# Two stages with fewer products on TensorE: a convolution mixer by one level of Strassen's scheme, and attention heads that scale probabilities on VectorE and fetch the rotated halves by DMA

## The chip, the cores and the metric

The kernel runs on one core of a Trainium2 chip. The time is device microseconds for one execution of the whole program; lower is better. Everything is computed in float32.

## The reference, cut to what matters

The program is a block of three mixers (window attention, a gated linear recurrence, a delta-rule recurrence) followed by two further layers on 1040 tokens (16 learned ones and the 1024 of the input), each a mixer and a mixture of 64 experts. The change touches the mixers of those two layers:

```python
def short_conv_mixer(hn, w_in, conv_w, w_out):      # hn: 1040 x 1024, w_in: 1024 x 3072
    bcu = hn @ w_in
    b, c, u = jnp.split(bcu, 3, axis=-1)
    z = c * u
    z = lax.conv_general_dilated(z, conv_w, ..., padding=((2, 0),), feature_group_count=z.shape[-1])  # 3 taps
    return (b * z) @ w_out

def apply_rope(x, cos, sin):
    x1, x2 = x[..., :half], x[..., half:]
    return jnp.concatenate([x1 * cos - x2 * sin, x1 * sin + x2 * cos], axis=-1)

# attention of layer 2: 8 heads, queries and keys of 128 plain + 64 rotated columns, values of 128
q = (cq @ w_uq).reshape(bsz, t, 8, 128 + 64)
q_rope = apply_rope(q[..., 128:], cos, sin)
s = (q_nope @ k_nope.T + q_rope @ k_rope.T) * scale, causal
o = softmax(s, axis=-1) @ v
```

## The kernel before

The program is a chain of phases. A phase holds its tiles and semaphores, runs one program on each engine, and ends in a barrier of all engines. Within a phase each engine works through its own list in order and waits on semaphores. The order of the work is written by hand. SyncE (SP) issues the loads; at the end of a phase's list it issues the first loads of the next one (`next_loads`). Activations lie transposed in one big tile `all__arena` (feature on the partitions, token along the row).

**`conv_mixer` (phase cm, tiles `cm__...`).** The features of the output come in 8 tiles `j` of 128, each with three sets `s` (b, c, u). The tokens are cut in three (`CUTS`: 352, 352 and 336 columns). For each `j` and cut, TensorE makes 3 products (b, c, u), each a sum over 8 tiles `k` of the input feature: 8 x 3 x 3 x 8 = 576 matmuls (line 1514). In the trace a float32 matmul of 128 rows shows as two MATMUL records and two LDWEIGHTS records. ScalarE copies b and c out of PSUM (lines 1529, 1530), VectorE multiplies c by u (L1542), and when a whole `j` is there it applies the three taps (L1545 and twice L1547) and the gate b (L1550). Two PSUM groups of three banks alternate. The weights of tile `j` (1.5 MB) are loaded two tiles ahead into one of two buffers; those of tile 0 are loaded by the phase before, `first_out`, in the list of SyncE between the store of row tile 2 and the load of row tile 4.

**`heads` (phase hd, tiles `hd__...`).** The eight heads are done in four pairs `j`. For a pair, TensorE first runs 14 jobs (`job`, L1674): four for the plain queries (`qn`), four for the rotated ones (two halves of the tokens, each once with the weights as they are, `qa`, and once with weights whose halves are exchanged, `qb`), each 3 matmuls of 512 columns, and six for the keys (`kn`), each 2 matmuls of 352 or 336 columns. VectorE takes each result out of its PSUM bank (`job_out`): for `qa` it multiplies by the cosines (L1837), for `qb` by the sines and adds (L1839, L1840). There are four banks, so job n waits until job n-4 was taken out. The values follow (L1684, 256 columns). Then come 8 units `n`, one for each block of 128 queries, the longest first (i = 7 down to 0, with 16 + 128(i+1) keys). TensorE's list for them is `score(n+1)`, then for both heads `turn(n, h)` (transposes of the probabilities, L1727) and for both heads `mix(n, h)` (probabilities times values, L1737). `mix` ends with one more matmul, of `ones` by a diagonal matrix `dg` that holds the reciprocals of the row sums (L1739), which spreads them over all partitions. `score(n+1)` waits until both exponentials of unit n are done, since it writes the banks that these read.

ScalarE's list is `evacuate(n-1, 0)` (copies of the turned probabilities, L1798, L1802), `exponentials(n, 0)` (L1785), `evacuate(n-1, 1)`, `exponentials(n, 1)`. VectorE's list is `biggest(n)` (mask L1858, maximum L1864, L1867), `output(n-1)` (copy of the spread reciprocals L1885, product with the mixed values L1886), `diagonals(n)` (reciprocal L1878, diagonal L1879). Before the last `turn` and `mix` of a pair, TensorE already does the first two jobs of the next pair (`EARLY`).

## Time and profile before

| | |
|---|---|
| time, median of 3 runs | 3213.69 us (3211.97 to 3217.08) |
| the profiled execution, its own time | 3214.27 us |
| its span, first to last instruction | 3212.5 us |
| mean granted TensorE clock | 0.931 of 2.4 GHz |
| busy in the span | TensorE 88%, VectorE 31%, ScalarE 18%, GpSimd 6% |
| phase cm, first to last matmul | 849.5 to 1187.6 us |
| phase hd, first matmul to last output | 2026.0 to 2471.0 us |

Times are microseconds from the start of the span unless marked ns. PE is TensorE's matmuls, PEld its weight loads (they run beside the matmuls), DVE VectorE, ACT ScalarE, POOL GpSimd, SPq the DMA queue of SyncE. The start-to-start distance of matmul records, not the duration of one, tells how fast TensorE goes, since they overlap. PEclk is the granted clock as a share of 2.4 GHz: 0.50 is the level of 1.2 GHz.

### The profile page before, as it was taken

How to read it: one execution, taken by the hardware profiler on the slowest of the kernel's cores; microseconds unless marked ns; L12 is line 12 of the kernel's file. 1: busy time of each engine (PE TensorE's matmuls, PEld its weight loads, DVE VectorE, ACT ScalarE, POOL GpSimd, SP SyncE). 2: the span in 40 equal slices, each digit the busy share in tenths (PEclk: the TensorE clock that was granted, in tenths of full speed). 3: DMA queues.
4: the chain of work that ended last, by engine and by line, in shares of the span. 5: the costliest groups of instructions: out<-in, count | busy, mean ns of one | idle time of the engine just before them, and what ended most of it. 6: DMA issues, size and time to landing. Idle time of an engine off the chain costs nothing. (4 is left out here: it accounts for less than half of the span.)

```text
span 3212.5 us, 31853 instructions
## 1 busy us (share of the span) xinstructions
PE 2825.0 (88%) x12118; PEld 1575.5 (49%) x12118; DVE 990.6 (31%) x2388; ACT 586.7 (18%) x1370; POOL 205.1 (6%) x331
## 2 busy tenths in 40 slices
PE   9999988989899989988887859899999979787882
PEld 3445588874466655533333326566656543333330
DVE  2423845544311113421110124344343442011114
ACT  0211544331000001111110113123112111111111
POOL 1000011110000000011111100000000001111110
PEclk9999988889899999988998979999999979899896
DMA  2111010002111204479999973002000549999995
GB/s 101 40 33 40 1 40 0 0 27 100 52 40 40 114 1 169 186 313 420 420 420 419 418 293 145 17 1 93 1 1 1 203 185 391 420 420 419 418 412 213
DMA packets 104902, 563.98 MB, mean 176 GB/s; under 512 B 20897, under 2 KB 21057, under 8 KB 52401
## 3 DMA queue, kind: packets, MB, share of 16 engines
q1 hardware_dynamic: 78432, 500.83, 38.9%
q0 software_dynamic: 21440, 43.51, 3.6%
...
## 5 line engine op out<-in xcount | busy, mean ns | idle before, releaser
L2005 PE MATMUL ex__h_ps<-all__arena,ex__xT 128*64 128x512 f32 x1696 | 526.8, 676 | 169.2 <-DMA all__arena<-in_w_up 113.9
L2005 PEld LDWEIGHTS ex__h_ps<-all__arena,ex__xT 128*64 128x64 f32 x1696 | 171.3, 155 | 471.4 <-issue 467.1
L1514 PE MATMUL cm__acc<-all__arena,cw__w 128*128 128x352 f32 (+1 forms) x1152 | 338.5, 457 | 2.3 <-PEq L81 2.3
L295 PE MATMUL fr__acc<-X__xT,fr__w 128*128 128x512 f32 x640 | 280.0, 598 | 7.8 <-DMA X__xT<-in_xT 7.8
L1514 PEld LDWEIGHTS cm__acc<-all__arena,cw__w 128*128 128x128 f32 x1152 | 220.2, 191 | 120.4 <-issue 4.6
L1302 PE MATMUL pb__acc<-b__w,all__arena 128*128 128x512 f32 x544 | 246.1, 607 | 12.5 <-POOL pb__eps L1256 12.5
L2033 DVE TENSOR_TENSOR ex__hs<-ex__sg,ex__h_ps 128x256 f32<-128x256 f32 x64 | 27.0, 421 | 680.6 <-ACT ex__sg L2030 680.3
L295 PEld LDWEIGHTS fr__acc<-X__xT,fr__w 128*128 128x128 f32 x640 | 121.8, 191 | 163.7 <-issue 155.4
L2005 PE MATMUL ex__h_ps<-mo__wx,ex__xT 128*64 128x512 f32 x352 | 177.0, 661 | 0.0
L1302 PEld LDWEIGHTS pb__acc<-b__w,all__arena 128*128 128x128 f32 x544 | 103.2, 194 | 132.9 <-issue 119.3
L2019 PE MATMUL ex__y_ps<-b__w,ex__hT 128*64 128x512 f32 x672 | 153.5, 598 | 1.1 <-ACT ex__hT L2036 1.1
L2030 ACT ACTIVATE ex__sg<-ex__h_ps 128x256 f32<-128x256 f32 x64 | 24.6, 384 | 656.4 <-PE ex__h_ps L2005 656.4
L1737 PE MATMUL hd__o<-all__arena 128*128 128x128 f32 (+1 forms) x704 | 102.6, 285 | 4.0 <-ACT all__arena L1802 4.0
L1542 DVE TENSOR_TENSOR cm__z<-cm__cT,cm__acc 128x352 f32<-128x352 f32 (+1 forms) x24 | 12.4, 516 | 293.2 <-ACT cm__cT L1530 293.2
L2042 DVE COPY ex__ysb<-ex__y_ps 128x512 f32<-128x512 f32 x64 | 44.3, 692 | 189.1 <-PE ex__y_ps L2019 189.1
L2154 POOL DMA_INDIRECT b__rows<-s_hn,mo__queue x60 | 60.6, 1009 | 614.9 <-PE ex__x_ps L1998 614.9
L1998 PEld LDWEIGHTS ex__x_ps<-mo__ident,b__rows 128*128 128x128 f32 x512 | 63.2, 195 | 66.2 <-issue 66.2
L1737 PEld LDWEIGHTS hd__o<-all__arena 128*128 128x128 f32 (+1 forms) x704 | 88.1, 190 | 15.5 <-ACT all__arena L1802 7.5
L1069 PE MATMUL fo__acc<-all__arena 128*128 128x512 f32 x192 | 88.2, 610 | 2.4 <-PEq L81 2.4
L1998 PE MATMUL ex__x_ps<-mo__ident,b__rows 128*128 128x128 f32 x512 | 75.7, 292 | 15.6 <-PEq L81 15.6
L1674 PE MATMUL hd__s<-lt__cq,lt__wq 128*128 128x512 f32 x192 | 85.1, 601 | 2.8 <-POOL hd__ones L1648 2.8
L2159 POOL DMA_INDIRECT s_ys<-ex__ysb,mo__queue x64 | 65.2, 1019 | 289.6 <-DVE ex__ysb L2042 285.9
...
## 6 DMA issues: line engine op xcount, KB each, us to landing
...
b__w<-in_w_down SPq DMA_DIRECT2D x84, 1024.0 KB, 20.5
...
```

The lines of the kernel that those rows point to most:

```text
L295: last = mm(acc[:, b, c], wbuf[:, b, k], xT[:, k, 512 * c:512 * c + 512], start=(k == 0), stop=(k == KT - 1))
L1069: last = nc.tensor.matmul(acc[:, t % 2, c], proj[:, G_T + k, P * t:P * t + P], wo[k][:, 512 * c:512 * c + 512], start=(k == 0), stop=(k == ...
L1302: last = mm(acc[:, t % 2, c], src[:, k, P * t:P * t + P], w[:, k, 512 * c:512 * c + 512], start=(k == 0), stop=(k == KT - 1))
L1514: last = nc.tensor.matmul(acc[:, u % 2, s, 0:cols], w[:, j % 2, s, k], hnT[:, k, at:at + cols], start=(k == 0), stop=(k == KT - 1))
L1674: last = mm(job_bank(n)[:, 0:cols], w[:, j % 2, k, which], src[:, k, at:at + cols], start=(k == 0), stop=(k == kt - 1))
L1737: mm(o_ps[:, h, 0:P], vv[0:r, s, h], pT[0:r, h, s], start=(a == 0), stop=(a == len(tiles) - 1))
L1998: last = nc.tensor.transpose(x_ps[:, k // 4, P * (k % 4):P * (k % 4) + P], xe[:, b, k::KT], ident[:])
L2005: last = nc.tensor.matmul(h_ps[half, b].rearrange("p (a b) -> p a b", a=2), xT[:, b, k, half], slots[n][:, :, k], start=(k == 0), stop=(k ...
L2019: last = nc.tensor.matmul(y_ps[half, c], hT[:, b, k, half], slots[n][:, k, 512 * c:512 * c + 512], start=(k == 0), stop=(k == 1))
L2042: return nc.vector.tensor_copy(ysb[:, b, 512:], y_ps[:, 1])
L2154: g.indirect_dma_start(xe[:, p % 2], None, hn_dram[:, :], bass.IndirectOffsetOnAxis(ap=queue[:, 0, p:p + 1], axis=0), bounds_check=T - 1, ...
L2159: g.indirect_dma_start(y_rows[:, :], bass.IndirectOffsetOnAxis(ap=queue[:, 1, p:p + 1], axis=0), ysb[:, p % 2], None, bounds_check=2 * T - ...
```

## The change

**`conv_mixer`.** The output is made in units (`CONV_UNITS`), each for two neighbouring output tiles and one set s: 4 x 3 = 12 units, in the order c, u, b. A unit is a product of a 2 x 2 block matrix of weights (two output tiles by two halves of the input features) and a 2 x 2 block matrix of activations (two halves of the input features by two halves of the tokens, 520 each). It is computed in the form of Strassen's scheme that has seven products and needs sums of blocks ahead of them and behind them. The halves of the tokens are cut in two again, so that a step `u` (24 of them) has seven products of 4 matmuls with 260 columns: 24 x 7 x 4 = 672 matmuls. VectorE makes four sums of weights for a unit (`weight_sums`, 128 x 512 each), four sums of activations for each half (`row_sums`, 4 x 260 columns each, once), and seven sums of 260 columns for a step, each with one operand in PSUM (`first_sums`, `last_sums`). ScalarE copies the first product of each step. The seven products of a step go through the eight PSUM banks in turn, so a product waits for the sum that reads the product eight before it. The gate and the taps work on two output tiles at once or are spread between the sums. The weights have three buffers of 1 MB, and `first_out` now loads the first three units (6 DMAs, 3 MB) where it loaded tile 0 (3 DMAs, 1.5 MB).

**`heads`.** The two `qb` jobs of a pair are gone, and the rotated queries come first. Their result is copied to `raw`; four DMAs of SyncE (32 partitions, 128 KB each) write it to `rot` with the halves exchanged (`exchange`), and VectorE forms raw x cos + rot x sin over 1024 columns in three steps behind jobs 3, 4 and 5 (`rotate`). The matmul of `ones` and `dg` is gone. VectorE instead multiplies the probabilities of a unit by the reciprocals of their row sums, in place, before they are turned (`norms`, 128 x number of keys), `turn` waits for that, and the output is a copy. `norms(n)` stands ahead of `output(n-1)` in VectorE's list. In SyncE's list `exchange(1)` and `exchange(2)` stand behind the weight loads of pairs 2 and 3, and `exchange(3)` ahead of `next_loads`. The reordered columns of the query weights are left out, so that a pair's weights are 3 instead of 4 tiles for each k.

```diff
+CONV_SETS = (1, 2, 0)
+CONV_UNITS = [(i, s) for i in range(KT // 2) for s in CONV_SETS]
+TH = T // 2
+TC = TH // 2
+HK = KT // 2
+def conv_weight(sp, D, w, loaded, n):
+    i, s = CONV_UNITS[n]
+    for m in range(2):
+        sp.dma_start(w[:, n % 3, m], D["conv_w_in_t"][2 * i + m, :, s]).then_inc(loaded[n % 3], 16)
...
+        sums = ph.sb("sums", [P, 2, 3, HK, P])
+        t4 = ph.sb("t4", [P, HK, TH])
+        z = ph.sb("z", [P, 2, 2, T + 2])
+        ub = ph.sb("ub", [P, 2, T])
+        acc = ph.ps("acc", [P, 8, 512])
...
+        M1, M5, M6, M7, M2, M4, M3 = range(7)
+        U2, W, C22, V5, C11, C21, C12 = range(1, 8)
+        bank = lambda u, x: acc[:, (7 * u + x) % 8, 0:TC]
...
+                for n in range(3, NU):
+                    sp.wait_ge(product, 14 * (n - 2))
+                    conv_weight(sp, D, w, w_loaded, n)
...
+                def mul(u, x, weight, moving, c):
+                    for k in range(HK):
+                        last = nc.tensor.matmul(bank(u, x), weight(k), moving(k, c), start=(k == 0), stop=(k == HK - 1))
+                    last.then_inc(product, 1)
...
+                for n in range(NU):
+                    r, q = n % 3, n % 2
+                    pe.wait_ge(w_loaded[r], 32 * (n // 3 + 1))
+                    a11, a12, s3, a22 = (lambda k, m=m, h=h: w[:, r, m, HK * h + k] for m, h in ((0, 0), (0, 1), (1, 0), (1, 1)))
+                    s1, s2, s4 = (lambda k, x=x: sums[:, q, x, k] for x in range(3))
...
+                        u = 2 * n + c
                         if u >= 2:
-                            pe.wait_ge(z_made, u - 1)
-                            pe.wait_ge(copied, u - 1)
-                        for s in range(3):
-                            if u == 0:
-                                pe.wait_ge(part_loaded[s], 16)
-                            for k in range(KT):
-                                last = nc.tensor.matmul(acc[:, u % 2, s, 0:cols], w[:, j % 2, s, k],
-                                                        hnT[:, k, at:at + cols], start=(k == 0), stop=(k == KT - 1))
-                        last.then_inc(done, 1)
+                            pe.wait_ge(summed, 7 * (u - 2) + C12)
+                        mul(u, M1, a11, b11, c)
+                        pe.wait_ge(s_made, 4 * n + 1)
+                        pe.wait_ge(t_made, 4 * c + 1)
+                        if u:
+                            pe.wait_ge(e1_out, u)
+                        mul(u, M5, s1, t1, c)
+                        pe.wait_ge(s_made, 4 * n + 2)
+                        pe.wait_ge(t_made, 4 * c + 2)
+                        if u:
+                            pe.wait_ge(summed, 7 * (u - 1) + V5)
+                        mul(u, M6, s2, t2, c)
+                        pe.wait_ge(s_made, 4 * n + 3)
+                        pe.wait_ge(t_made, 4 * c + 3)
+                        mul(u, M7, s3, t3, c)
+                        mul(u, M2, a12, b21, c)
+                        if u:
+                            pe.wait_ge(summed, 7 * (u - 1) + C11)
+                        pe.wait_ge(t_made, 4 * c + 4)
+                        mul(u, M4, a22, t4n, c)
+                        if u:
+                            pe.wait_ge(summed, 7 * (u - 1) + C21)
+                        pe.wait_ge(s_made, 4 * n + 4)
+                        mul(u, M3, s4, b22, c)
...
+                for u in range(2 * NU):
+                    act.wait_ge(product, 7 * u + M1 + 1)
+                    if u >= 2:
+                        act.wait_ge(summed, 7 * (u - 2) + C11)
+                    nc.scalar.copy(e1[:, u % 2], bank(u, M1)).then_inc(e1_out, 1)
...
+                def weight_sums(n, *which):
+                    r, q = n % 3, n % 2
+                    a11, a12, a21, a22 = (w[:, r, m, HK * h:HK * h + HK] for m, h in ((0, 0), (0, 1), (1, 0), (1, 1)))
+                    if 1 in which:
+                        dve.wait_ge(w_loaded[r], 32 * (n // 3 + 1))
+                        v(V.tensor_tensor(sums[:, q, 0], a21, a22, ALU.add))
+                        dve.sem_inc(s_made, 1)
...
+                def row_sums(c, *which):
+                    lo, hi = low(c), high(c)
+                    if 1 in which:
+                        v(V.tensor_tensor(t12[:, 0, :, lo], B12[:, :, hi], B11[:, :, lo], ALU.subtract))
+                        dve.sem_inc(t_made, 1)
...
+                def add(u, result, out, a, b, op=ALU.add):
+                    V.tensor_tensor(out, a, b, op).then_inc(summed, 1)
+                    dve.wait_ge(summed, 7 * u + result)
...
+                    dve.wait_ge(e1_out, u + 1)
+                    dve.wait_ge(product, 7 * u + M6 + 1)
+                    add(u, U2, u2, e1[:, u % 2], bank(u, M6))
+                    dve.wait_ge(product, 7 * u + M7 + 1)
+                    add(u, W, c21, u2, bank(u, M7))
+                    add(u, C22, c22, c21, bank(u, M5))
+                    add(u, V5, c12, u2, bank(u, M5))
...
+                    dve.wait_ge(product, 7 * u + M2 + 1)
+                    add(u, C11, c11, e1[:, u % 2], bank(u, M2))
+                    dve.wait_ge(product, 7 * u + M4 + 1)
+                    add(u, C21, c21, c21, bank(u, M4))
+                    dve.wait_ge(product, 7 * u + M3 + 1)
+                    add(u, C12, c12, c12, bank(u, M3))
...
+                def gated(n, i):
+                    v(V.tensor_tensor(z[:, i % 2, :, 2:2 + T], z[:, i % 2, :, 2:2 + T], ub[:], ALU.mult))
...
+                weight_sums(0, 1)
+                row_sums(0, 1)
+                weight_sums(0, 2)
+                row_sums(0, 2)
+                weight_sums(0, 3)
+                row_sums(0, 3, 4)
+                weight_sums(0, 4)
+                for i in range(KT // 2):
+                    nc_, nu, nb = 3 * i, 3 * i + 1, 3 * i + 2
+                    end = i == KT // 2 - 1
+                    first_sums(nc_, i, 1, 0)
+                    if i == 0:
+                        row_sums(1, 1, 2, 3, 4)
+                    last_sums(nc_, i, 1, 0)
+                    weight_sums(nu, 1, 2, 3, 4)
+                    first_sums(nc_, i, 1, 1)
+                    last_sums(nc_, i, 1, 1)
+                    first_sums(nu, i, 2, 0)
+                    last_sums(nu, i, 2, 0)
+                    weight_sums(nb, 1, 2, 3, 4)
+                    first_sums(nu, i, 2, 1)
+                    last_sums(nu, i, 2, 1)
+                    gated(nu, i)
+                    if i == 0:
+                        dve.wait_ge(taps_loaded, 16)
+                    tap(i, 0, 0)
...
+                    first_sums(nb, i, 0, 0)
+                    tap(i, 0, 1)
+                    tap(i, 0, 2)
+                    last_sums(nb, i, 0, 0)
+                    if end:
+                        tap(i, 1, 0)
+                        tap(i, 1, 1)
+                    else:
+                        weight_sums(nb + 1, 1, 2, 3, 4)
+                    first_sums(nb, i, 0, 1)
+                    if end:
+                        tap(i, 1, 2)
+                    else:
+                        tap(i, 1, 0)
+                        tap(i, 1, 1)
+                    last_sums(nb, i, 0, 1)
+                    if not end:
+                        tap(i, 1, 2)
+                    v(V.tensor_tensor(zT[:, 2 * i:2 * i + 2, 0:T], zT[:, 2 * i:2 * i + 2, 0:T], ub[:], ALU.mult))
...
-        rot = carve(512)
+        raw = ph.sb("raw", [P, SEQ])
+        rot = ph.sb("rot", [P, SEQ])
...
-        jobs = ([("qn", h, c) for h in range(2) for c in range(2)] + [(kind, 0, c) for c in range(2) for kind in ("qa", "qb")]
+        jobs = ([("qr", 0, c) for c in range(2)] + [("qn", h, c) for h in range(2) for c in range(2)]
...
+                def exchange(j):
+                    sp.wait_ge(raw_out, 2 * (j + 1))
+                    for at in range(0, P, ROPE):
+                        for a, b in ((at, at + ROPE // 2), (at + ROPE // 2, at)):
+                            sp.dma_start(rot[a:a + ROPE // 2], raw[b:b + ROPE // 2]).then_inc(exchanged, 16)
+                exchange(0)
                 for j in range(2, NPAIR):
                     sp.wait_ge(pdone, NJ * (j - 1))
                     sp.wait_ge(v_done, NV * (j - 1))
                     pre.pair(sp, j)
+                    exchange(j - 1)
+                exchange(NPAIR - 1)
...
-                    pe.wait_ge(exped, 2 * u + h + 1)
+                    pe.wait_ge(normed, 2 * u + h + 1)
...
-                        mm(o_ps[:, h, 0:P], vv[0:r, s, h], pT[0:r, h, s], start=(a == 0), stop=(a == len(tiles) - 1))
-                    pe.wait_ge(diag_done, 2 * u + h + 1)
-                    mm(o_ps[:, h, P:2 * P], ones[:], dg[:, h, u % 2], start=True, stop=True).then_inc(mixed, 1)
+                        last = mm(o_ps[:, h, 0:P], vv[0:r, s, h], pT[0:r, h, s], start=(a == 0), stop=(a == len(tiles) - 1))
+                    last.then_inc(mixed, 1)
...
-                        act.wait_ge(diag_done, 2 * (u - 2) + h + 1)
...
-                        elif kind == "qa":
-                            if j == 0:
-                                dve.wait_ge(tab_loaded, 32)
-                            v.hold(tt(qr[:, cols], job_bank(n), cosT[:, cols], ALU.mult))
                         else:
-                            v(tt(rot[:], job_bank(n), sinT[:, cols], ALU.mult))
-                            v.hold(tt(qr[:, cols], qr[:, cols], rot[:], ALU.add))
+                            v(V.tensor_copy(raw[:, cols], job_bank(n)))
+                            dve.sem_inc(raw_out, 1)
...
+                def rotate(j, step):
+                    if step == 0:
+                        if j == 0:
+                            dve.wait_ge(tab_loaded, 32)
+                        v.hold(tt(qr[:], raw[:], cosT[:], ALU.mult))
+                    elif step == 1:
+                        dve.wait_ge(exchanged, 64 * (j + 1))
+                        v.hold(tt(rot[:], rot[:], sinT[:], ALU.mult))
+                    else:
+                        v(tt(qr[:], qr[:], rot[:], ALU.add))
...
-                def diagonals(j, n):
+                def norms(j, n):
                     i, u = units[n], NB * j + n
                     p = u % 2
                     for h in range(2):
                         dve.wait_ge(exped, 2 * u + h + 1)
                         if i == NB - 1:
                             v(tt(ls[:, h, p, 0:1], ls[:, h, p, 0:1], ls[:, h, p, 1:2], ALU.add))
-                        if u >= 2:
-                            dve.wait_ge(mixed, 2 * (u - 2) + h + 1)
                         v(V.reciprocal(rl[:, h, p:p + 1], ls[:, h, p, 0:1]))
-                        V.tensor_scalar(dg[:, h, p], ident[:], rl[:, h, p:p + 1], None, ALU.mult).then_inc(diag_done, 1)
+                        keys = keys_of(i)
+                        V.tensor_scalar(pr[:, h, p, 0:keys], pr[:, h, p, 0:keys], rl[:, h, p:p + 1], None,
+                                        ALU.mult).then_inc(normed, 1)
                 def output(j, n):
                     i, u = units[n], NB * j + n
                     for h in range(2):
                         dve.wait_ge(mixed, 2 * u + h + 1)
-                        v(V.tensor_copy(ob[:, h], o_ps[:, h, P:2 * P]))
-                        tt(oT[:, 2 * j + h, P * i:P * i + P], o_ps[:, h, 0:P], ob[:, h], ALU.mult).then_inc(oout, 1)
+                        V.tensor_copy(oT[:, 2 * j + h, P * i:P * i + P], o_ps[:, h, 0:P]).then_inc(oout, 1)
...
+                        if 3 <= n <= 5:
+                            rotate(j, n - 3)
                     values_out(j, 0)
                     biggest(j, 0)
                     for g in range(1, NV):
                         values_out(j, g)
-                    diagonals(j, 0)
+                    norms(j, 0)
                     for n in range(1, NB):
                         biggest(j, n)
+                        norms(j, n)
                         output(j, n - 1)
-                        diagonals(j, n)
```

## Rows read from the trace of the kernel before

**Rows 1.** The page, its head: the span.

```profile
span 3212.5 us, 31853 instructions
```

**Rows 2.** Windows: us, busy time (count) of PE, PEld, DVE, ACT, POOL, granted clock, DMA.

```profile
850.00:854.00 4.00, 4.00 (x8) 2.25 (x8) 0.57 (x2) 0.00 (x0) 0.00 (x0) 0.50 0.80 271
...
849.50:1187.60 338.10, 338.07 (x1152) 220.18 (x1152) 44.94 (x53) 18.36 (x46) 0.00 (x0) 0.99 0.14 51
...
330.00:410.00 80.00, 76.39 (x531) 43.00 (x529) 64.25 (x156) 51.17 (x160) 2.23 (x7) 1.00 0.00 1
...
2026.00:2471.00 445.00, 423.37 (x2064) 274.46 (x2064) 190.62 (x556) 99.97 (x305) 0.39 (x2) 1.00 0.05 20
```

**Rows 3.** Groups by shape, 845 to 1195 us: count, busy, mean ns, idle before.

```profile
L1514 PE MATMUL cm__acc<-all__arena,cw__w 128*128 128x352 f32 x768 | 231.1, 463 | 2.3 <-PEq L81 2.3
L1514 PEld LDWEIGHTS cm__acc<-all__arena,cw__w 128*128 128x128 f32 x1152 | 220.2, 191 | 120.4 <-issue 4.6
...
L1547 DVE SCALAR_TENSOR_TENSOR all__arena<-cm__z,cm__taps,all__arena 128x1040 f32<-128x1040 f32 x16 | 20.8, 1301 | 0.6
L1550 DVE TENSOR_TENSOR all__arena<-all__arena,cm__bT 128x1040 f32<-128x1040 f32 x8 | 9.9, 1241 | 0.3
...
L1545 DVE TENSOR_SCALAR all__arena<-cm__z,cm__taps 128x1040 f32<-128x1040 f32 x8 | 6.1, 761 | 0.3
```

**Rows 4.** Timeline, first and last of phase cm: start, us, engine, line.

```profile
849.53 16.71 PE L1514 MATMUL cm__acc<-all__arena,cw__w 128*128 128x352 f32 x47 [2.26 <-PEq L81]
...
850.50 0.06 DVE L1536 MEMSET cm__z<- 128x4 f32 x1
...
1188.05 0.44 ACT L1529 COPY cm__bT<-cm__acc 128x336 f32<-128x336 f32 x1 [12.75 <-PE cm__acc L1514]
...
1192.88 1.24 DVE L1550 TENSOR_TENSOR all__arena<-all__arena,cm__bT 128x1040 f32<-128x1040 f32 x1
```

**Rows 5.** Timeline, VectorE elsewhere: two-source operations of other widths.

```profile
702.89 0.42 DVE L764 TENSOR_TENSOR rwc__gr<-rwc__y,V__dg 128x256 f32<-128x256 f32 x1 [0.71 <-PE rwc__y L890]
...
2043.91 0.69 DVE L1840 TENSOR_TENSOR all__arena<-all__arena 128x512 f32<-128x512 f32 x1
...
278.06 2.29 DVE L472 TENSOR_TENSOR all__arena<-all__arena,fr__cum 128x2048 f32<-128x2048 f32 x1
```

**Rows 6.** Timeline, PE in phase hd: runs of matmuls of one width.

```profile
2048.13 7.16 PE L1674 MATMUL hd__s<-lt__ckv,lt__wkv 128*128 128x352 f32 x24
...
2165.71 1.89 PE L1684 MATMUL hd__t<-lt__wkv,lt__ckv 128*128 128x256 f32 x8
...
2174.17 3.72 PE L1684 MATMUL hd__t<-lt__wkv,lt__ckv 128*128 128x256 f32 x16
...
2245.65 5.32 PE L1674 MATMUL hd__s<-lt__cq,lt__wq 128*128 128x512 f32 x12
```

**Rows 7.** Timeline, PE and ACT around the seventh unit of a pair (i = 1).

```profile
2238.87 0.18 ACT L1785 ACTIVATION_READ_ACCUMULATOR all__arena<-hd__s,hd__nm 128x1 f32 x1
...
2239.25 1.25 PE L1737 MATMUL hd__o<-all__arena 128*128 128x128 f32 x8
...
2240.43 0.49 PE L1739 MATMUL hd__o<-hd__dg,hd__ones 128*128 128x128 f32 x2
...
2240.75 0.66 PE L1708 MATMUL hd__s<-all__arena 128*128 128x144 f32 x4
...
2241.78 0.87 PE L1727 MATMUL hd__t<-hd__ident,all__arena 128*128 128x128 f32 x6
```

**Rows 8.** Timeline, PE, a mix of 18 records and what follows it.

```profile
2190.38 2.42 PE L1737 MATMUL hd__o<-all__arena 128*128 128x128 f32 x18
2192.73 0.49 PE L1739 MATMUL hd__o<-hd__dg,hd__ones 128*128 128x128 f32 x2
```

**Rows 9.** Groups by line, 2024 to 2475 us.

```profile
L1879 DVE TENSOR_SCALAR hd__dg<-hd__ident,hd__rl 128x128 f32<-128x128 f32 x64 | 18.4, 287 | 2.3
```

**Rows 10.** DMA issues: destination and source, queue, count, size, us to landing.

```profile
all__arena<-all__arena SPq DMA_DIRECT2D x2, 256.0 KB, 6.2
```

127 lines of the change are left out of this document (66 added, 61 removed).

## The prediction

> **What bounds the kernel now.** I read the page first for the span [rows 1], then windows over the two phases that change [rows 2], then the groups by shape and the timeline inside them. In the convolution phase TensorE is busy 338.07 of 338.10 us, in the heads phase 423.37 of 445.00, both near the full clock; VectorE works 44.9 and 190.6 us there, the DMA engines 14% and 5% of the time [rows 2]. Both phases are streams of matmuls, and what they lose or gain moves all that follows, since each ends in a barrier; the weights of the experts, which fill the DMA engines later, are asked for only behind those barriers. So a matmul taken out of these two phases is worth its full distance to the next, unless its replacement makes TensorE wait.
>
> **What a column costs.** 24 records of 352 columns take 7.16 us. A record's own duration is 0.463 us [rows 3], which is its columns and 0.17, so the distance is (7.16 - 0.46) / 23 = 0.291 us. For 12 records of 512 columns it is (5.32 - 0.59) / 11 = 0.430 [rows 6]. Both are 0.83 ns per column and record, which is two passes at 2.4 GHz. The narrowest run of similar width has 256 columns: 8 records, (1.89 - 0.39) / 7 = 0.214, again 0.83 ns per column; in a run of 16 records over more groups, (3.72 - 0.39) / 15 = 0.222 [rows 6]. A weight load of 0.191 us [rows 3] thus stays hidden behind 256 columns; at 128 it no longer does: 18 and 8 records take 2.35 and 1.18 us, 0.117 apart where the columns need 0.107 [rows 7, 8].
>
> **Convolution, TensorE.** Before: 1152 records of 346.7 columns on average, 332.8 us at 0.833 ns; measured 338.1, the 5.3 us more mostly the start at the lower level of the clock, 0.50 until about 854 [rows 2, 4]. After: 672 matmuls, 1344 records of 260 columns, 291.2 us. That is -41.6 us. The bounds of the seam between products: nothing, as in the 256-column run of 8, or 0.222 - 0.214 = 0.008 us a record, +10.8 us. The 352-column run crosses six groups with their semaphores at 0.291, so I take the near end, +1.5.
>
> **Convolution, VectorE.** It must not hold TensorE. An operation of two sources costs 0.42 us at 256 columns, 0.69 at 512, 1.24 at 1040, 2.29 at 2048; the one-source tap 0.76, the other two taps 1.30 [rows 3, 5]; behind each I add 0.04 for the wait on itself. Sums behind products: 24 x 7 x 0.46 = 77 us. Sums of weights: 12 x 4 x 0.73 = 35. Sums of activations: 8 x 1.28 = 10. Gates: 8 operations of 2080 columns at 2.35 = 19. Taps: 8 x (0.80 + 2 x 1.34) = 28. Together 169 us of 291, so what counts is the order. A step on TensorE lasts 7 x 1.73 = 12.1 us. Its products end at 1.7, 3.5, 5.2, 6.9, 8.7, 10.4 and 12.1; VectorE's first four sums run from 5.2 to 8.3, its last three end at 9.1, 10.9 and 12.6. The sum on which the next step depends first (V5) is there at 8.3 and wanted at 12.1 + 3.5 = 15.6. The heaviest stretch lies behind every sixth step: a tap and the gate, 1.34 + 2.35, from 12.6 to 16.3, where the next sums may start at 17.3. Four weight sums (2.9 us) fit at the other places, and they are wanted one step later. ScalarE has one copy a step. So no wait in steady state: 0.
>
> The start is tight. Matmuls begin at 849.5, VectorE is free at 850.6 behind its memsets [rows 4]. It makes the sums in pairs of 0.73 + 1.28 = 2.0 us: ready at 852.6, 854.6, 856.6. The first product runs at half the clock, 8 x 0.433 = 3.5 us, so the second wants its pair at 853.0, the third at about 855.4, the fourth at 857.2. Each is ready 0.4 to 0.8 us ahead; if the operations on three-dimensional views are slower, the loss is one or two us, and a clock that rises sooner costs as much. I take +0.3.
>
> **Convolution, the end.** From the last copy's start (1188.05) to the end of VectorE (1192.88 + 1.24 = 1194.12) it now takes 6.1 us [rows 4]: two copies, a product, three taps and the gate. After, the taps are done, and one sum and the gate remain: 0.46 + 2.35 = 2.8. That is -3.3. Convolution: -41.6 + 1.5 + 0.3 - 3.3 = -43.1 us.
>
> **Loads.** The first three units are 3 MB in place of 1.5 ahead of the load of row tile 4 in `first_out`. Three more DMAs of 512 KB delay that load by the time of 1.5 MB; the rows give 4.00 us at 271 GB/s for 1.1 MB [rows 2], so some 5.5 us. A row tile on TensorE there is 32 records of 512 columns, 13.7 us, and tile 4 is two tiles off: hidden. Later units are asked for two units ahead, 48 us. Without that cover: +5.5, once.
>
> **Heads, the jobs.** Two jobs of 3 matmuls fewer in each of 4 pairs: 4 x 12 records x 0.430 = -20.6 us. VectorE's share is 0.69 + 1.28 behind jobs 3 to 5, under the 2.58 us of a job, so no bank is late. The exchange: four DMAs of 128 KB; the nearest row is a pair of 256 KB with 6.2 us to landing [rows 10]. At the first pair `raw` is ready after two jobs and its copy, and VectorE asks for the result behind job 4, 2.5 jobs or 7 us later; there TensorE can go on for four jobs before a bank is missing, 2.6 + 3 x 1.2 = 6 us more. So 13 us of cover at the first pair, 15 at the others, where the two early jobs come ahead of the last turn. Behind the waiting VectorE stand the outputs of later jobs, nothing else. Bounds: 0, or at a landing of 20 us 4 x 6 = +24 us. I take 0. On SyncE `exchange(3)` now stands before `next_loads`, which so slip by about a pair and a half; a pair of some 100 us is left for 6 MB: 0. The loads of pairs 2 and 3 are ahead of their exchanges or wait for the previous one, still a pair early: 0.
>
> **Heads, the spreading matmul.** 64 times two records. In their place they take 0.32 us from their start to the next [rows 7]; at the distance of the neighbours 2 x 0.117 = 0.234. So -15.0 to -20.5 us; the row of the operation itself is nearer, I take 0.30: -19.2.
>
> **Heads, scaling the probabilities.** A one-source operation goes from 0.287 us at 128 columns [rows 9] to 0.761 at 1040 [rows 3], 0.52 ns a column. Mean 592 keys: 0.53 us, 64 times 34 us, against the diagonal (0.29) and one of two output operations (0.29), 37 us, that go. VectorE's load stays. The latency falls between exponential and turn. TensorE runs `score(n+1)` there: the last exponential of unit 6 ends at 2239.05, the score starts at 2240.75 and the turn at 2241.78 [rows 7]. The scaling needs 0.2 + 0.35 us for 272 keys and is through at 2239.6. Earlier units have longer scores. Without a score as cover is only the last unit of the last pair: +0.3 at most (the others have early jobs of 5.1 us). Cover gone everywhere: 64 x 0.75 = +48. The output is one operation shorter at the phase's end, -0.3; `ones` is not awaited, -0.1. Together 0.
>
> Heads: -20.6 - 19.2 = -39.8; I leave +0.3 for the last unit: -39.5.
>
> **A rule against it.** In the heads phase TensorE is idle for 445.0 - 423.4 = 21.6 us in many short waits, and the granted clock is 1.00 all the same; with VectorE 80% busy it is 1.00 too [rows 2]. The Trainium skill, page "TensorE: Matmul & The Clock Gate", section "A second HAM failure mode: psum-queue depth-cycling", tells of a kernel that cycles through PSUM banks and pauses between its groups, so that the clock swings between its two levels. By the row the sum has no term for it; by the rule it is the third rival below.
>
> **The sum.** 3214.3 (the profiled execution, 3212.5 of it span) - 43.1 - 39.5 = 3131.7. The median of the runs is 0.6 us lower, so 3131.
>
> **Rivals.** *First: the products wait for sums.* Every sum is a separate VectorE instruction, and each product has its wait. For it: the tight start. Against it: after the start each sum is ready 4 us or more ahead of the product that wants it, by the list above. If each of the 168 products waited 0.25 us, the convolution's gain would be gone: 3131 + 43 = 3174. *Second: heads gain nothing,* since the exchange or the scaling holds TensorE: 3131 + 39.5 = 3171. Against it: 13 us of cover and the score between. *Third, slower: the clock falls in the convolution.* Short waits between products of 1.7 us bring the level of 0.50, which the trace shows only at the phase's start, behind a barrier [rows 2]. At that level the phase's 291 us of matmuls cost 291 more: 3422 if it holds throughout; from 82.6 / 291 = 28% of the matmuls on the kernel is slower than before. (This is what the page above would give.) *Fourth: nothing comes of it,* both first rivals in full: 3214.
>
> **Chances.** Forecast 0.80, with a range of its own from 3119 (seams nothing, the spreading matmul at its full 0.32, a bit less waiting on ScalarE) to 3147 (seams 10.8, spreading matmul at 0.234, some us of waits). First rival 0.07, second 0.05, third 0.04, fourth 0.01; still faster than 3119, 0.03. The measurement tells 0.2%, 6 us, from no change. Faster 0.95, same 0.01, slower 0.04. The range is 3119 to 3151: it takes in a small part of the first two rivals.
>
> **What would show it.** Convolution: 1344 records 0.217 us apart, from first to last about 296 us, VectorE near 169 us busy, granted clock as before, some 3 us from the last matmul to the end. Wrong if TensorE shows idle time between the products, released by VectorE's sums, or a clock of 0.5 beyond the first 5 us. Heads: about 405 us, with no wait of TensorE for VectorE's scaling and VectorE's wait for the exchange under a job's length. Wrong if the jobs of a pair are pulled apart or `turn` waits for the reciprocals. Elsewhere nothing should move by more than 2 us.

## The result and the profile after

The changed kernel takes 3136.01 us (median, 3133.99 to 3136.61) against 3212.83 us beside it on the same chip: a ratio of 0.9758, interval 0.9741 to 0.9775. It is faster, as forecast, and 3136 lies inside the forecast's own range of 3119 to 3147, 5 us above the predicted 3131. The profiled execution is the fastest of its four, 3133.99 us; the page's head (it answers to [rows 1]):

```profile
span 3132.2 us, 32250 instructions
```

Windows of the changed kernel over the first 4 us of convolution, its matmuls, and the heads' matmuls (the columns are those of [rows 2]):

```profile
850.00:854.00 4.00, 4.00 (x11) 3.05 (x10) 3.56 (x6) 0.38 (x1) 0.00 (x0) 0.50 0.04 7
849.05:1146.40 297.35, 297.35 (x1344) 257.33 (x1344) 158.06 (x256) 9.02 (x24) 0.00 (x0) 0.99 0.15 53
1981.21:2391.00 409.79, 388.21 (x1888) 251.05 (x1888) 191.97 (x488) 99.53 (x305) 0.39 (x2) 1.00 0.08 26
```

The convolution's matmuls are one unbroken stream again, 297.35 us busy of 297.35, with VectorE at 158 us in place of 45 (the window ends before its last sum and gate, 2.7 us more). In the heads TensorE has 35 us less to do and the same idle time.

To see where the time went I cut both traces at the first matmul of four phases: convolution, the mixture of experts behind it, heads, the second mixture.

| us | before | after | difference | forecast |
|---|---|---|---|---|
| up to convolution | 849.53 | 849.05 | -0.5 | 0 |
| convolution, to the next phase's first matmul | 347.49 | 303.23 | -44.3 | -43.1 |
| from there to the heads | 828.99 | 828.93 | -0.1 | 0 |
| heads, to the next phase's first matmul | 447.82 | 412.30 | -35.5 | -39.5 |
| the rest | 738.72 | 738.72 | 0.0 | 0 |
| span | 3212.5 | 3132.2 | -80.3 | -82.6 |

So the gain sits in the two edited phases, and the 2.3 us by which this execution missed the sum are errors of opposite sign: 1.2 us more in the convolution, 4.0 us less in the heads, and 0.5 us that came before either.

The medians fell by 76.8 us only, 3.5 less than the two profiled executions differ. The stretch up to the convolution takes 847.2 to 851.6 us in the 14 profiles of this document. One part of that is 3.4 us at the granted clock of 0.50 within the program's first phase: 9 of the 10 profiles with the new convolution have it and 1 of the 4 with the old one. Whether that is chance or follows from the change the runs don't show; it is worth 1.7 us, and the account below is of the two phases alone.

**Convolution.** Groups by shape of the changed kernel, 849 to 1152 us (they answer to [rows 3]):

```profile
L1533 PE MATMUL cm__acc<-all__arena,cw__w 128*128 128x260 f32 x576 | 136.0, 386 | 2.3 <-PEq L81 2.3
L1533 PE MATMUL cm__acc<-all__arena,cm__sums 128*128 128x260 f32 x576 | 134.9, 384 | 0.0
L1533 PE MATMUL cm__acc<-cm__t,cw__w 128*128 128x260 f32 x192 | 46.0, 383 | 0.0
L1656 DVE SCALAR_TENSOR_TENSOR all__arena<-cm__z,cm__taps,all__arena 128x1040 f32<-128x1040 f32 x16 | 20.8, 1302 | 0.6
...
L1622 DVE TENSOR_TENSOR cm__ub<-cm__ub,cm__acc 128x260 f32<-128x260 f32 x48 | 20.4, 425 | 27.6 <-PE cm__acc L1533 26.8
...
L1649 DVE TENSOR_TENSOR cm__z<-cm__z,cm__ub 128x2080 f32<-128x2080 f32 x4 | 9.3, 2325 | 0.1
...
L1590 DVE TENSOR_TENSOR cm__sums<-cw__w 128x512 f32<-128x512 f32 x12 | 8.3, 692 | 0.4
...
L1605 DVE TENSOR_TENSOR all__arena<-all__arena 128x1040 f32<-128x1040 f32 x2 | 2.5, 1242 | 0.2
```

Idle time stands on the side of VectorE (it waits for products), none on TensorE's but the 2.3 us in which its sequencer leaves the barrier. All prices of VectorE are those of the forecast: 0.425, 0.692, 1.242, 2.325 us. Its 169 counted the 0.04 us behind each instruction, which is no busy time: 256 x 0.04 = 10 us of what 158 lacks to it.

The start, in the timeline of the changed kernel:

```profile
849.05 3.81 PE L1533 MATMUL cm__acc<-all__arena,cw__w 128*128 128x260 f32 x8 [2.26 <-PEq L81]
...
850.84 1.24 DVE L1605 TENSOR_TENSOR all__arena<-all__arena 128x1040 f32<-128x1040 f32 x1
...
852.65 4.46 PE L1533 MATMUL cm__acc<-all__arena,cm__sums 128*128 128x260 f32 x16
...
853.06 1.24 DVE L1608 TENSOR_TENSOR all__arena<-all__arena 128x1040 f32<-128x1040 f32 x1
```

The first row sum ends at 852.08 and is wanted at 852.65; the second ends at 854.30 and the third product starts behind the second's eight records, without a bracket of idle time. And the end:

```profile
1144.49 1.92 PE L1533 MATMUL cm__acc<-all__arena,cm__sums 128*128 128x260 f32 x8
...
1146.51 0.42 DVE L1622 TENSOR_TENSOR cm__ub<-cm__ub,cm__acc 128x260 f32<-128x260 f32 x1 [1.33 <-PE cm__acc L1533]
1146.97 2.32 DVE L1706 TENSOR_TENSOR all__arena<-all__arena,cm__ub 128x2080 f32<-128x2080 f32 x1
...
1152.28 1.22 PE L1302 MATMUL pb__acc<-b__w,all__arena 128*128 128x512 f32 x1 [5.88 <-POOL pb__eps L1256]
```

One sum and one gate remain, and the next phase's matmul finds TensorE idle for 5.88 us, where it was 9.00 (1188.02 to 1197.02).

**Heads.** The waits of TensorE in the changed kernel, 1981 to 2393 us (total, times, longest):

```profile
PE hd__t L1889 <- ACT all__arena L1958: 8.9, 20, 0.6
PE hd__t L1889 <- ACT all__arena L1962: 4.1, 8, 0.7
PE hd__o L1899 <- ACT all__arena L1962: 4.0, 12, 0.3
PE hd__t L1846 <- DVE all__arena L2016: 4.0, 4, 1.0
PE hd__s L1836 <- POOL hd__ident L922: 2.7, 1, 2.7
```

No line names the exchange or the scaling (L2046). The first four stand in the kernel before with the same figures. The exchange, from the timeline, and its group of DMAs:

```profile
1988.05 0.69 DVE L1995 COPY hd__raw<-hd__s 128x512 f32<-128x512 f32 x1 [1.78 <-PE hd__s L1836]
1988.83 2.49 SPq L1796 DMA_DIRECT2D hd__rot<-hd__raw  x4
...
1996.62 1.22 DVE L2008 TENSOR_TENSOR hd__rot<-hd__rot,lt__sinT 128x1024 f32<-128x1024 f32 x1
```

```profile
hd__rot<-hd__raw SPq DMA_DIRECT2D x8, 128.0 KB, 2.5
```

Four issues take 2.49 us, and each 128 KB lands some 2.5 us behind its issue: by the landings in the trace all is there at 1993.06, 4.3 us behind the second copy to `raw` (4.2 to 5.1 us over the four pairs), and VectorE asks at 1996.62. The Trainium skill, page "SBUF — State Buffer", section "The DMA setup-cost knee", gives about 2 us of fixed cost and a rate that approaches 436 GB/s, an estimate of 2.3 us or more here; the trace's 2.5 agrees.

**The clock at a phase's start.** Windows over the heads' first microseconds, the changed kernel and then the same kernel profiled again:

```profile
1981.21:1984.00 2.79, 2.79 (x4) 1.24 (x5) 0.00 (x0) 0.59 (x1) 0.39 (x2) 0.50 0.00 0
1984.00:1986.00 2.00, 2.00 (x6) 0.94 (x5) 0.42 (x1) 0.00 (x0) 0.00 (x0) 0.99 0.00 0
```

```profile
1983.73:1989.00 5.27, 5.27 (x6) 2.19 (x7) 0.00 (x0) 0.59 (x1) 0.39 (x2) 0.50 0.00 0
1990.00:1992.00 2.00, 2.00 (x6) 0.81 (x5) 0.05 (x1) 0.00 (x0) 0.00 (x0) 1.00 0.00 0
```

TensorE begins the heads at 1.2 GHz (0.50), straight after 2.67 us of idle time at the barrier, and stays there for 2.8 us in one execution and 6.1 in another of the same kernel. Half of that time is lost, and what is lost differs by 1.6 us for no reason that lies in the code. Below, the "clear" length of the heads is the phase's length less half the time at 0.50 at its start. It tells 0.1 us: 410.88 and 410.89 in the two executions of the changed kernel. It leaves in it what is lost at the phase's end, where two of the kernels below come to 0.50 before their last matmul. In the convolution the level of 0.50 lasted 5.2 us in every profile, 2.6 us lost.

### The profile page after: what moved, and what is told of

Its sections match the earlier page's. It is cut to its first block and busy times, and to the rows that moved or that the text cites. A ratio compares the mean times of both kernels' runs of the same rounds, so it can differ in the third digit from the quotient of the medians.

```text
span 3132.2 us, 32250 instructions
## 1 busy us (share of the span) xinstructions
PE 2744.9 (88%) x12134; PEld 1586.8 (51%) x12134; DVE 1102.6 (35%) x2520; ACT 575.6 (18%) x1346; POOL 205.0 (7%) x330
## 5 line engine op out<-in xcount | busy, mean ns | idle before, releaser
L1533 PE MATMUL cm__acc<-all__arena,cw__w 128*128 128x260 f32 x576 | 136.0, 386 | 2.3 <-PEq L81 2.3
L1533 PE MATMUL cm__acc<-all__arena,cm__sums 128*128 128x260 f32 x576 | 134.9, 384 | 0.0
L1533 PEld LDWEIGHTS cm__acc<-all__arena,cw__w 128*128 128x128 f32 x576 | 110.6, 192 | 19.7 <-issue 2.6
L1533 PEld LDWEIGHTS cm__acc<-all__arena,cm__sums 128*128 128x128 f32 x576 | 110.3, 191 | 17.0
L2211 DVE COPY ex__ysb<-ex__y_ps 128x512 f32<-128x512 f32 x64 | 44.3, 692 | 189.4 <-PE ex__y_ps L2188 189.4
```

Source lines behind the costliest of these rows:

```text
L1533: last = nc.tensor.matmul(bank(u, x), weight(k), moving(k, c), start=(k == 0), stop=(k == HK - 1))
L2211: return nc.vector.tensor_copy(ysb[:, b, 512:], y_ps[:, 1])
```

## The experiments

All lengths of phases, from the profile of each kernel:

| kernel | convolution | heads | at 0.50 | heads, clear |
|---|---|---|---|---|
| before | 347.49 | 447.82 | 2.9 | 446.37 |
| after | 303.23 | 412.30 | 2.8 | 410.88 |
| after, again | 303.23 | 413.95 | 6.1 | 410.89 |
| convolution's edit alone | 303.24 | 449.35 | 6.1 | 446.31 |
| exchange alone | 347.48 | 428.69 | 5.9 | 425.75 |
| scaling alone | 347.47 | 434.50 | 6.1 | 431.45 |
| old convolution, 260 columns | 348.23 | 449.03 | 5.5 | 446.30 |
| sums issued twice | 304.35 | 412.47 | 3.1 | 410.91 |
| exchange as 16 DMAs | 303.24 | 415.60 | 2.8 | 414.18 |
| no scaling | 303.24 | 412.36 | 2.9 | 410.89 |
| scaling late | 303.23 | 416.28 | 6.2 | 413.17 |
| shared bank, two turn banks | 303.23 | 414.63 | 6.1 | 411.60 |
| shared bank, three turn banks | 303.22 | 400.31 | 2.9 | 398.84 |
| the same, identity awaited late | 303.24 | 400.08 | 3.6 | 398.27 |

**1. The convolution's edit alone.** `conv_mixer`, `conv_weight` and the buffers around them as after, `heads` as before.

> The convolution mixer in the seven-product form, the heads as before. Theory A (each phase is a stream of matmuls between two barriers, its gain is its own and moves the rest rigidly): from the first matmul of the convolution to the first matmul behind its barrier 303 us instead of 347.5, so 44 us less, 3168 to 3169 us in all; heads phase 447.8 us as before. Rival B (part of the gain seen in the convolution hangs on something else, such as the smaller head weights or the later loads): a different length of the phase, over 305 us, or a total above 3171.

3171.97 us, ratio 0.9869 (0.9852 to 0.9885). The phase has the length of the full change to 0.01 us, and the clear heads that of before to 0.1 us. The total is 3 us longer than the first theory said and above the 3171 that rival B named. Its phases don't bear the rival out: against the kernel before, the profiled execution reaches the convolution 1.8 us later (851.30) and loses 1.6 us more at the heads' slow start. The kernel before, run beside it, took 3214.51 us, and the 44.3 us of the phase lie inside the interval of the ratio.

**2. The exchange alone.** The convolution as before; `heads` takes 3 columns of query weights, `raw`, the DMAs and `rotate`; the diagonals stay.

> Convolution as before; in the heads only the exchanged halves by DMA and two jobs fewer a pair; the matmul of ones and the diagonal stays. Theory A: 48 records of 512 columns less at 0.430 us, so 20.6 us off the heads phase (427.2 us from its first matmul to the first behind the barrier, before 447.8), total 3192. Rival B (the wait for the exchange costs something that the scaling of probabilities hides, or the start of a pair is bound by VectorE): a gain under 18 us, and TensorE or VectorE waiting for the exchange.

3195.78 us, ratio 0.9943 (0.9926 to 0.9960). Clear heads 20.6 us shorter: 446.37 - 425.75. The total is 4 us above the 3192 expected, against 3214.51 us for the kernel before; 20.6 us lie inside the interval of the ratio.

**3. The scaling alone.** The diagonals and the spreading matmul go, `turn` waits for the scaling, which stands ahead of the output; all else is as before:

```diff
-                    pe.wait_ge(diag_done, 2 * u + h + 1)
-                    mm(o_ps[:, h, P:2 * P], ones[:], dg[:, h, u % 2], start=True, stop=True).then_inc(mixed, 1)
+                    last.then_inc(mixed, 1)
...
-                        V.tensor_scalar(dg[:, h, p], ident[:], rl[:, h, p:p + 1], None, ALU.mult).then_inc(diag_done, 1)
+                        keys = keys_of(i)
+                        V.tensor_scalar(pr[:, h, p, 0:keys], pr[:, h, p, 0:keys], rl[:, h, p:p + 1], None,
+                                        ALU.mult).then_inc(diag_done, 1)
```

> Convolution and rotated queries as before; in the heads only the scaling of probabilities on VectorE ahead of the turn, without the matmul of ones and the diagonal. Theory A1: the 128 records are worth the distance of their neighbours, 0.117 us each, and the seam of 0.1 us a unit that they hid comes back in front of the score: 15.0 us off, heads phase 432.8 us, total 3198. Theory A2 (my prediction's term): 0.30 us for each pair of records, 19.2 us off, 428.6 us; then the missing 4 us in the changed kernel belong to the rotated queries. Rival: a wait of TensorE for the scaling, gain under 13 us.

3201.57 us, ratio 0.9963 (0.9949 to 0.9978), against the expected 3198; the interval holds the 14.9 us by which the clear heads are shorter. The two halves together make 35.5 us, as the full change has: they don't touch each other. So the spreading matmul was worth the lower bound of its range, 15.0. Set side by side record by record, the two traces show how the 14.9 come about. In each of 64 places 0.325 us go from the start of the removed pair of records to the start of what follows it. But in 62 of them the next record, the first of a mix or of a score, is now 0.21 us from the one behind it, where it was 0.11 or 0.12. In the mixes, records of 128 rows are 0.112 us apart, and the last two of each have 16 rows (the learned tokens) and stand 0.20 to 0.21 us apart; the first record behind them of 128 rows does too, whichever it is. That is 64 x 0.325 - 62 x 0.10 = 14.5 us, and the last 0.4 lie at the end of the phase.

**4. The old convolution, 260 columns.** The scheme of before, but four cuts of 260 columns in place of three of 352, 352 and 336. It is about the 5 us that the convolution had over its columns.

```diff
+CUTS4 = [(260 * n, 260) for n in range(4)]
...
-                    for n, (at, cols) in enumerate(CUTS):
+                    for n, (at, cols) in enumerate(CUTS4):
```

> The kernel before, with the tokens of the convolution cut in four times 260 columns instead of 352, 352 and 336: 768 matmuls, 1536 records, in 96 groups of 16 records. It asks where the 0.0025 us over the 0.2167 us of 260 columns come from that the changed kernel shows a record. If they belong to each record of this width: 0.2192 us a record, 336.7 us and the slow start of 2.4. If they belong to each product (0.020 us at a change of PSUM bank with its semaphore): 0.2179 us a record, 334.7 us. If they come only from VectorE's sums: 332.8 us. The whole kernel within 0.2% of before in each case.

One run, 3213.44 us. The window over its matmuls:

```profile
848.81:1188.24 339.43, 339.43 (x1536) 293.54 (x1536) 46.24 (x61) 20.26 (x62) 0.00 (x0) 0.99 0.14 51
```

The same columns, a third more records, 0.9 us longer. Less the last record's own 0.39 and the 2.59 lost to the clock, 336.45 us over 1535 distances is 0.2192. For the changed kernel it is 294.37 / 1343 = 0.2192; for before, whose matmuls reach from 849.53 to 1188.02, (338.49 - 0.46 - 2.59) / 1151 = 0.2914 at 346.7 columns. Each is its columns at 0.8333 ns and 2.5 ns more: 216.7 + 2.5, 288.9 + 2.5. The old scheme has 16 records in an accumulation and the new one 8, so the 2.5 ns belong to the record and not to the seam between products. The Trainium skill says so too, page "TensorE: Matmul & The Clock Gate", section "Wait — 56ns, not 53.3ns?": about 2.5 ns for each matmul at the full clock, whatever its width. The trace agrees; its unit here is the record, of which an f32 matmul has two.

**5. Every sum behind a product issued twice.** Is the order of VectorE tight? The first copy goes into a scratch tile.

```diff
+        again = ph.sb("again", [P, TC], mybir.dt.bfloat16)
...
                 def add(u, result, out, a, b, op=ALU.add):
 
+                    v(V.tensor_tensor(again[:], a, b, op))
                     V.tensor_tensor(out, a, b, op).then_inc(summed, 1)
```

> Convolution phase with every one of the 168 sums behind a product issued twice, the first time into a scratch tile. VectorE's work there rises by 168 x 0.43 = 72 us, from 158 to 230 of 297. Theory A (VectorE is hidden in steady state, as the list of times in the prediction has it): TensorE waits nowhere but at the start, the end is 0.4 us later, convolution 303.2 to 305. Rival (the order of VectorE is already tight, and each product waits for a sum): the work added shows in part, 0.2 us or more a product, convolution 335 or longer, with TensorE idle behind the sums.

VectorE's work went to 232 us of 303, from 161 us in the same window of the changed kernel, and TensorE's busy stretch didn't move; window of this kernel, 849 to 1152 us, and the wait behind the phase:

```profile
849.00:1152.00 303.00, 296.95 (x1344) 256.62 (x1343) 232.27 (x429) 9.01 (x24) 0.57 (x4) 0.99 0.15 52
```

```profile
PE pb__acc L1302 <- POOL pb__eps L1256: 7.0, 1, 7.0
PE cm__acc L1534 <- PEq L81: 2.3, 1, 2.3
```

The phase grew by 1.1 us, all of it in the wait at its end (7.0 for 5.9), where sums stand behind the last products. The steady state takes 71 us more of VectorE for nothing: the first rival is out with room to spare.

**6. The exchange as 16 DMAs.** How long is its cover? The same bytes in 16 pieces of 8 partitions, VectorE waiting for all.

```diff
-                            sp.dma_start(rot[a:a + ROPE // 2], raw[b:b + ROPE // 2]).then_inc(exchanged, 16)
+                            for r in range(0, ROPE // 2, 8):
+                                sp.dma_start(rot[a + r:a + r + 8], raw[b + r:b + r + 8]).then_inc(exchanged, 16)
```

> The exchange of the rope queries' halves as 16 DMAs of 8 partitions in place of four of 32, the same bytes. Issued one behind the other at some 0.6 us each, the last is out 10 us behind the raw queries and has landed some 12.5 us behind them, in place of 4.9. Theory A (the cover is as long as the trace shows, some 7.8 us from the raw queries to VectorE's question at the first pair, and TensorE has three more jobs before it lacks a bank): VectorE waits some 5 us at the first pair, TensorE at most 2 us, the other pairs likewise or less: total at most 2 to 4 us longer in the heads. Rival (the prediction's second: the exchange holds TensorE): each pair is later by 4 us or more, heads 16 us longer.

Clear heads 3.3 us longer. The first pair, in the timeline of this kernel:

```profile
1991.01 10.84 SPq L1797 DMA_DIRECT2D hd__rot<-hd__raw  x16
...
2003.59 1.23 DVE L2009 TENSOR_TENSOR hd__rot<-hd__rot,lt__sinT 128x1024 f32<-128x1024 f32 x1 [4.94 <-DMA hd__rot<-hd__raw]
...
2005.53 0.86 PE L1837 MATMUL hd__s<-lt__ckv,lt__wkv 128*128 128x352 f32 x2 [1.53 <-DVEq L1999]
```

The raw queries are ready at 1990.92 and VectorE asks at 1998.65, 7.7 us later; then it waits 4.94 us. Set side by side with the changed kernel, record by record, TensorE loses 2.55 us for it, in two waits of which the lines show the first. At the third pair VectorE waits 3.07 us and TensorE loses 0.72; at the two others VectorE waits 2.1 us and TensorE loses nothing. That is the whole 3.3 us, and each time TensorE loses what VectorE waits beyond 2.4 us. So the cover at the first pair is 7.7 + 2.4 = 10.1 us; the prediction had 13. The exchange as built is in by 5.1 us and well under it.

**7. The scaling left out, and the scaling late.** Two kernels bound what the scaling costs. The first drops the multiplication of the probabilities (its outputs are not normalized):

```diff
-                        v(V.reciprocal(rl[:, h, p:p + 1], ls[:, h, p, 0:1]))
-                        keys = keys_of(i)
-                        V.tensor_scalar(pr[:, h, p, 0:keys], pr[:, h, p, 0:keys], rl[:, h, p:p + 1], None,
-                                        ALU.mult).then_inc(normed, 1)
+                        V.reciprocal(rl[:, h, p:p + 1], ls[:, h, p, 0:1]).then_inc(normed, 1)
```

> The changed kernel with the 64 multiplications of the probabilities left out (the outputs are then not divided by their sums of exponentials): the turn waits for the reciprocal alone. Lengths of the heads phase are told without the time that the clock's start costs; the changed kernel has 411.0 us by it. Theory A (the scaling lies under the next unit's score, by the prediction's step): 410 to 411 us, at most 1 us shorter, which is the last unit of the last pair. Rival (it costs latency at each unit): each of the 32 units loses 0.2 to 0.5 us by it, so the phase is 6 to 16 us shorter without it, 395 to 405.

410.89 us clear, the same to 0.01 us. The second puts it behind the output of the unit before:

```diff
                     for n in range(1, NB):
                         biggest(j, n)
-                        norms(j, n)
                         output(j, n - 1)
+                        norms(j, n)
```

> VectorE takes the output of unit n - 1 ahead of the reciprocals and the scaling of unit n, in place of behind them. The scaling can then start only when TensorE has mixed unit n - 1, and nothing but the score of unit n + 1 covers it: after the last mix 0.29 (output) + 0.20 (reciprocal) + 0.30 to 0.76 (scaling) us, against a score of 1.1 us at the shortest. Theory A: the score covers it, heads 411 to 413 us. Rival (the waits add up to more than the score, by semaphores between the steps): 0.3 to 0.5 us a unit, 421 to 427 us.

413.17 us clear, 2.3 more and just over what the first theory allowed; one wait of TensorE for the scaling is long enough to be listed:

```profile
PE hd__t L1889 <- DVE all__arena L2046: 0.8, 1, 0.8
```

That is the last unit of the last pair, which has no score behind it, and the whole 2.3 us lie there; up to it no matmul is more than 0.1 us later than in the changed kernel, the slow start taken out. 0.9 us are the wait, and 1.4 us follow from the clock: the granted clock falls to 0.50 at 2392.0, behind that wait, and the last turn and mix run at that level. The window of this kernel:

```profile
2392.00:2396.00 4.00, 3.88 (x12) 2.29 (x12) 0.58 (x2) 0.82 (x4) 0.00 (x0) 0.50 0.00 0
```

As the kernel was changed even this unit is covered. The timeline of the changed kernel shows by what, at the last unit of the last pair:

```profile
2385.49 2.18 PE L1899 MATMUL hd__o<-all__arena 128*128 128x128 f32 x12 [0.33 <-ACT all__arena L1962]
...
2386.07 0.29 DVE L2046 TENSOR_SCALAR all__arena<-all__arena,hd__rl 128x144 f32<-128x144 f32 x1
...
2386.81 0.30 DVE L2046 TENSOR_SCALAR all__arena<-all__arena,hd__rl 128x144 f32<-128x144 f32 x1
...
2387.60 0.66 PE L1889 MATMUL hd__t<-hd__ident,all__arena 128*128 128x128 f32 x4
```

Both scalings are through at 2387.11, while TensorE still mixes the unit before, and the turn follows at 2387.60 without a wait. The cover is the mix and not only the score that the prediction named.

**8. Three banks for the turns.** Of the 23.7 us of listed waits in the heads, 17.0 are for one of the two banks of turned probabilities and values. There are eight banks, all in use; a third becomes free when both heads' outputs share one. Their readers then have to wait for both heads.

```diff
-        t_ps = ph.ps("t", [P, 2, 512])
-        o_ps = ph.ps("o", [P, 2, 512])
+        t_ps = ph.ps("t", [P, 3, 512])
+        o_ps = ph.ps("o", [P, 2, 256])
...
-                        if q >= 2:
-                            pe.wait_ge(turned_out, q - 1)
+                        if q >= 3:
+                            pe.wait_ge(turned_out, q - 2)
...
-                        pe.wait_ge(oout, 2 * (u - 1) + h + 1)
+                        pe.wait_ge(oout, 2 * u)
...
-                    act.wait_ge(maxed, 2 * u + h + 1)
+                    act.wait_ge(maxed, 2 * u + (2 if i == NB - 1 else h + 1))
...
-                        dve.wait_ge(mixed, 2 * u + h + 1)
+                        dve.wait_ge(mixed, 2 * u + 2)
```

The values take their bank by `g % 3` in the same way, and the tails of the two heads are made one behind the other.

> Heads phase with three banks in place of two for the turned probabilities and the values; the room comes from putting both heads' mixed outputs into one bank, whose readers then wait for both heads. Theory A: what is left of TensorE's idle time in this phase (8.9 us behind the larger evacuation, 4.1 and 4.0 behind the small one, 4.0 at the values) is mostly the wait for one of two banks; with a third, the waits of the turns after the first group of a unit go, and the values' wait: heads 5 to 13 us shorter, total 3123 to 3131. Rival: the waits are set by ScalarE's pace (a group of four transposes takes TensorE 0.5 us, its evacuation 0.6 to 0.7), so that a third bank only moves the wait one group on: total 3134 to 3136. Second rival, slower: the shared bank makes the mix of one unit wait for both outputs of the unit before, and VectorE is late with them: 32 units x 0.3 us = 10 us more, 3146.

3122.70 us (3119.38 to 3123.33), ratio 0.9709 (0.9693 to 0.9725), against 3138.66 us for the changed kernel run beside it:

> The changed kernel once more, unaltered, as the measure for the kernels of this call on the same chip. Both theories: 3136 us within 2 us, convolution 303 and heads 411 to 414 us. The granted clock at the start of each of the two phases is the one thing that may differ: it stayed at 0.50 for 2.6 us in one profile and for 6.0 in another, which is worth up to 1.7 us a phase.

Its ratio is 0.9760 (0.9744 to 0.9776), so the intervals don't meet. The clear heads are 12.05 us shorter. The waits of TensorE in the three-bank kernel:

```profile
PE hd__o L1901 <- ACT all__arena L1964: 4.0, 12, 0.3
PE hd__s L1836 <- POOL hd__ident L922: 2.7, 1, 2.7
PE hd__s L1872 <- ACT all__arena L1943: 2.2, 4, 0.6
PE hd__t L1891 <- ACT all__arena L1960: 1.8, 8, 0.3
```

Of the 17.0 us at turns and values 1.8 are left, and 2.2 us have come up anew at the score. Which half of the edit did it, the shared bank alone tells:

> The shared bank for both heads' outputs, but two banks for the turned probabilities as in the changed kernel: the half of the three-bank version that should cost, if anything. If the gain of that version (12.1 us in the heads phase) is the third bank's: 411 to 412 us here, with TensorE's waits behind the larger evacuation at 8.9 us as before. Rival: the gain came from the other order of waits at the mix, then 399 to 403 us here.

411.60 us clear, with the 8.9, 4.1, 4.0 and 4.0 us of waits unchanged. So the sharing costs 0.7 us and the third bank gives 12.8. (The three-bank kernel comes to 0.50 at 2376.75, in its last mix, which takes 2.33 us in place of 1.73; without that the third bank would have given 13.4.)

**9. The identity awaited late.** To this version, TensorE's wait for the identity moved to the first turn, VectorE's to the first maximum.

> The three-bank version, with TensorE's wait for the identity moved from the phase's start to the first turn, and VectorE's wait for mask and identity to the first maximum. The row shows 2.7 us of idle time of TensorE at the start, put down to GpSimd's identity; GpSimd itself starts only 0.7 us ahead of TensorE's first matmul, so most of it is the barrier. Theory A: 0.7 us less, heads 398 us, total 3122. Rival: all of the 2.7 us is the identity's, total 3120. Second rival: nothing, TensorE's own start behind the barrier is later than the identity.

The start in this kernel's timeline:

```profile
1982.90 0.20 POOL L920 MEMSET hd__ident<- 128x128 f32 x1 [42.12 <-POOLq L81]
...
1982.94 1.19 PE L1835 MATMUL hd__s<-lt__cq,lt__wq 128*128 128x512 f32 x1 [2.02 <-PEq L81]
```

TensorE is idle for 2.02 us in place of 2.67: the identity held it for 0.65 us, the rest is the barrier. This idle time lies ahead of the phase's first matmul, so the table's length of the heads doesn't hold it. That the clear length came out at 398.27, as the first theory had it, is luck: what it is shorter by, 0.6 us, is the last mix, which runs at the full clock here. The runs give 3121.98 us (3119.89 to 3125.35), ratio 0.9715 (0.9698 to 0.9731): no difference to the version above that they can tell.

## Why the prediction was right

**The convolution, TensorE: right, with two small terms wrong.** The columns give -41.6 as forecast. The seam of +1.5 does not exist: products follow each other without a gap, and there is instead 2.5 ns a record, which the kernel before paid too. Only 192 more records pay it now, +0.5. I had read the 5.3 us over the columns [rows 2] as "mostly the start at the lower level of the clock"; that start is 2.6 of them, the records 2.9. The cause of the misreading is a run in [rows 6]: the 24 records named 352 wide are 352, 352 and 336 wide, as in `CUTS`, and at their true mean of 346.7 columns their 0.2913 has the 2.5 ns in it. The 512-column run beside it has them too: 0.430 / 512 is 0.840 ns and not the 0.83 that I read. The +0.3 for the start was 0. Together -41.1 for -39.8.

**The convolution, VectorE and the end: right.** No wait in steady state, even with 71 us more work; the end gave -3.1 for -3.3. The 3 MB of first units ahead of `first_out`'s load cost nothing: that phase lasts 133.9 us from its first matmul to the convolution's in all 14 profiles, with 1.5 MB and with 3.

**The jobs: right.** -20.6 forecast, -20.6 measured with that half alone. The exchange lands in less than half the 6.2 us of its nearest row [rows 10] and stays hidden. Its cover was put too long, 13 us for 10.1: the 6 us of work that I left TensorE after VectorE's question counted banks alone. Behind the landing VectorE still multiplies (1.2 us) and copies the next job out (0.7 us) before a bank is free, and TensorE's real slack was 2.4 us.

**The spreading matmul: the term that was mis-sized.** The step was "the row of the operation itself is nearer, I take 0.30: -19.2". Measured: 14.5, and 14.9 with the phase's end, which I had booked under the scaling. The 0.32 in [rows 7] is right as what goes from that place, but 0.10 of it comes back at whatever follows, since the slow record behind the 16-row part of a mix was the spreading matmul's first and is now another's (experiment 3). The same unit of a pair in the changed kernel's timeline, the first pair here and the second in the rows:

```profile
2074.73 2.63 PE L1899 MATMUL hd__o<-all__arena 128*128 128x128 f32 x16 [0.33 <-ACT all__arena L1962]
...
2077.29 0.76 PE L1870 MATMUL hd__s<-all__arena 128*128 128x144 f32 x4
...
2078.42 0.88 PE L1889 MATMUL hd__t<-hd__ident,all__arena 128*128 128x128 f32 x6
```

From the score's start to the turn's it is now 1.13 us, where [rows 7] give 1.03. The two mixes take 2.56 us, 1.28 for each 8 records, where the one in [rows 7] that follows a spreading matmul takes 1.18. The whole miss in the heads, 4.0 us, is the 4.7 by which 14.5 falls short of 19.2, less the 0.3 that I had left for the last unit and the 0.4 at the phase's end.

**The scaling: right in its price, 0, and short in its reason.** The score is there as cover, but the mix of the unit before already does it. The +0.3 at the last unit did not come either, by the same cover; without it the last unit costs 0.9 us of waiting (experiment 7).

**The rivals.** The first (products wait for sums, 3174) falls with experiment 5. The second (heads gain nothing, 3171) falls with both halves measured alone and with the scaling left out; the exchange would begin to hold TensorE at a landing of 10 us. The third (the clock falls) did not come: 168 products walk through the eight banks in turn at a granted clock of 0.99 over the phase, the lower level in its first 5.2 us only, exactly as before. But its condition, short waits between the products, did not arise, so no run tested it. The same holds for the mechanism of the Trainium skill, page "TensorE: Matmul & The Clock Gate", section "A second HAM failure mode: psum-queue depth-cycling", which has TensorE idle briefly between its groups: this stream has no such idle time, 297.35 us busy of 297.35.
